# Index projection issued among the last filter sequences of the first stage, two filter layers stacked on 128 partitions, first tokens moved up

## What is computed

```python
# second block: filter network and spectra
hdn = concatenate([t, cos(bands * wpos), -sin(bands * wpos)])      # (1024, 33)
for k, w in enumerate((w_in, w_hid[0], w_hid[1])):                 # 33->64, 64->64, 64->64
    hdn = sin(freq[k] * (hdn @ w + b[k]))
h = (hdn @ w_out).reshape(L, 2, 2, 1024) * exp(-t * deltas)        # two orders, forward and backward
# ... rfft of the two-sided filters: L+1 frequencies, order, channel

# first block: E = 16 meta tokens + 1024 tokens
proj = h @ w_in                       # split into q_a, c_kv, q_idx, k_idx, w_idx, ..., i_h, ...
c = rms_norm(c_kv, kv_norm_g)         # latents (E, 128)
s_h = relu(q_idx @ k_idx.T * 64 ** -0.5)     # 4 index heads
s_idx = sum over heads of s_h * w_idx        # top 256 keys of each query are kept
```

## Time and profile before

| | us |
|---|---|
| median of three executions | 2971.05 (2970.11 to 2971.79) |
| profiled execution, device time | 2972.2 |
| its span in the trace | 2970.2 |
| filter network, until the first filter product on TensorE | 0 to 43.5 |
| sequences 0 to 7 and the stores | 43.5 to 337.5 |
| index projection stage | 337.5 to 386.2 |
| index scores stage | 386.2 to 413.9 |
| TensorE busy, whole span | 2660.5 (90%) |
| VectorE busy, whole span | 1870.5 (63%) |

### The profile page before, as it was taken

How to read it: one execution, slowest core, us unless ns; L and a number is a source line. 1 busy time by engine, 2 the same in 40 slices (tenths; PEclk the granted TensorE clock), 3 DMA queues, 4 the chain that set the end, 5 groups by cost and what they waited for, 6 DMA issues and landing times. The chain is left out here.

```text
span 2970.2 us, 30635 instructions
## 1 busy us (share of the span) xinstructions
PE 2660.5 (90%) x11185; PEld 1832.8 (62%) x11185; DVE 1870.5 (63%) x3013; ACT 927.1 (31%) x1681; POOL 865.8 (29%) x635
## 2 busy tenths in 40 slices
PE   5999789968599979789999999978999997999967
PEld 1444345557356557577787999976788884444456
DVE  6677279997676488657831555544764425887554
ACT  2121131101344333455425656644432220111132
POOL 0000000022121066675632333316532221333235
PEclk9999899989799989899999999998999998999979
DMA  5122301000100054246737231305321123111043
GB/s 165 64 78 85 122 23 36 28 37 1 57 1 1 1 199 135 77 136 219 256 129 232 61 93 48 93 22 169 127 80 43 43 78 152 46 60 60 29 177 106
DMA packets 110703, 265.01 MB, mean 89 GB/s; under 512 B 18387, under 2 KB 37531, under 8 KB 105952
## 3 DMA queue, kind: packets, MB, share of 16 engines
q1 hardware_dynamic: 110560, 263.13, 26.6%
HBM read 202.10 MB, written 60.99 MB: 89 GB/s over the span
## 5 line engine op out<-in xcount | busy, mean ns | idle before, releaser
L313 PE MATMUL psum<-part,part 128*128 128x512 f32 (+1 forms) x1984 | 764.6, 385 | 82.0 <-POOL part L1688 30.1
L314 PE MATMUL psum<-part,part 128*128 128x512 f32 (+1 forms) x1984 | 743.1, 375 | 0.0
L315 PE MATMUL psum<-part,part 128*128 128x512 f32 (+1 forms) x1984 | 741.2, 374 | 0.0
L1688 POOL TENSOR_TENSOR part<-arena,part 128x512 fp32r<-128x512 f32 (+1 forms) x298 | 427.1, 1444 | 631.2 <-ACT part L1682 630.9
L313 PEld LDWEIGHTS psum<-part,part 128*128 128x128 f32 x1984 | 378.4, 191 | 169.4 <-POOL part L1688 71.6
L314 PEld LDWEIGHTS psum<-part,part 128*128 128x128 f32 x1984 | 379.3, 191 | 70.5 <-issue 2.7
L315 PEld LDWEIGHTS psum<-part,part 128*128 128x128 f32 x1984 | 378.0, 191 | 71.7
L1682 ACT ACTIVATE part<-arena 128x512 fp32r<-128x512 f32 (+1 forms) x298 | 181.7, 620 | 364.4 <-PE psum L315 235.1
L221 PE MATMUL psum<-arena 128*128 128x512 f32 (+1 forms) x672 | 231.3, 504 | 17.8 <-DMA arena<-in_w_f 9.9
L1219 POOL TENSOR_TENSOR arena<-arena 128x256 f32<-128x256 f32 x56 | 39.2, 702 | 664.2 <-PE psum L1232 664.2
L2523 DVE TENSOR_REDUCE arena<-psum 128x1 f32<-128x1280 f32 x64 | 95.5, 1492 | 175.9 <-PE psum L2475 175.9
(11 more groups left out here) (326 smaller groups left out, 4112.4 us busy)
## 6 DMA issues: line engine op xcount, KB each, us to landing
arena<-in_ada_w SPq DMA_DIRECT2D x24, 1024.0 KB, 6.2
arena<-in_w_hy SPq DMA_DIRECT2D x40, 512.0 KB, 3.3
scratch_spec<-arena SPq DMA_DIRECT2D x68, 256.0 KB, 2.0
arena<-scratch_spec SPq DMA_DIRECT2D x12, 1024.0 KB, 5.2
arena<-in_w_gate SPq DMA_DIRECT2D x16, 512.0 KB, 4.0
arena<-in_w_out SPq DMA_DIRECT2D x16, 512.0 KB, 3.9
arena<-in_w_mgate SPq DMA_DIRECT2D x16, 512.0 KB, 4.0
arena<-in_w_mout SPq DMA_DIRECT2D x16, 512.0 KB, 3.9
```

Source lines behind the costliest of these rows:

```text
L313: nc.tensor.matmul(acc, a_hi, b_hi, start=start, stop=False)
L314: nc.tensor.matmul(acc, a_hi, b_lo, start=False, stop=False)
L315: return nc.tensor.matmul(acc, a_lo, b_hi, start=False, stop=stop)
L1688: self.K.nc.gpsimd.tensor_tensor(self.lo[s][:, c], self.raw[s][:, c], self.hi[s][:, c].bitcast(F32), ALU.subtract).then_inc(self.split, 1)
```

## The change

Four edits.

1. The stage `stage_index_projection` is gone. Its six products (`index_product(u)`, u = 0..5) are issued in `stage_spectra_tokens`: u = 0 at the start of sequence 6, u = 1 in its middle, u = 2 and u = 3 at the start and in the middle of sequence 7, u = 4 and u = 5 behind it. Each uses bank 6 or 7 and is copied out by ScalarE (`copy_index`). SyncE loads the index weights when the last token product is done, at its place in front of sequence 6. The latents are reloaded in `stage_index_scores`; the index head weights `wi` stay where they are made.
2. The first two layers of the filter network are stacked: both halves of the positions lie on 128 partitions, with block-diagonal weights, so a layer is one product, one reduction of seven instructions and one sine. The last layer stays in two halves. The network is 4 steps instead of 6.
3. Token tile 0 is multiplied in two parts ahead of and between the first filter products, tile 1 right behind them, and the others move up: the tables are now tiles 3, 4, 5, 6, 7 at the start of sequences 1 to 5, and tiles 2 and 8 in the middle of sequences 0 and 5. Sequences 6 and 7 have no token tile; `norm_latents` and its square root move from sequence 7 to sequence 6.
4. The sums and the rest of the second half's output weights move behind `fold_odd(0)` and into sequence 2 on VectorE, their rounding into sequence 1 on ScalarE. The loads are reordered: input and token weights come ahead of the transform's matrices.

```diff
-    AT_START = {0: 0, 1: 2, 2: 4, 3: 5, 4: 6, 5: 7, 6: 8}
-    AT_MIDDLE = {0: 1, 1: 3}
+    AT_START = {1: 3, 2: 4, 3: 5, 4: 6, 5: 7}
+    AT_MIDDLE = {0: 2, 5: 8}
+    INDEX_START, INDEX_MIDDLE, INDEX_END = {6: [0], 7: [2]}, {6: [1], 7: [3]}, [4, 5]
...
+    LAYERS = [(0, 0), (1, 0), (2, 0), (2, 1)]
...
+            def load_index(m):
+                if m == 2:
+                    sp.wait_ge(idx_mm, 2)
+                sp.dma_start(w_idx[m % 2], dram["w_idx"][m, :, :]).then_inc(idx_in[m % 2], 16)
...
+                if k == 6:
+                    sp.wait_ge(i_mm, 9)
+                    load_index(0)
+                    load_index(1)
+                if k == 7:
+                    load_index(2)
...
             rest_of_weights(0)
...
+            take_latent(0)
             for k, (o, h, s) in enumerate(ORDER):
...
-                if k == 0:
-                    sum_weights(1)
+                if k == 2:
                     rest_of_weights(1)
-                if k == 7:
+                if k == 6:
                     norm_latents()
...
+                if k == 0:
+                    take_latent(1)
...
                 fold_odd(K, dve, link, ed, odd, Y, s, y_ready)
+                if k == 0:
+                    sum_weights(1)
...
+            def copy_index(u):
+                act.wait_ge(idx_mm, u + 1)
...
+                for u in INDEX_START.get(k, []):
+                    copy_index(u)
...
-                if k == 7:
+                if k == 6:
                     act.wait_ge(meansq, 1)
                     a(rstd[:, 1:9], rstd[:, 1:9], ACT.Sqrt)
...
-            for q in range(4):
-                hidden_out(0, q)
+            token_products(0, 0)
+            hidden_out(0, 0)
+            hidden_out(0, 1)
+            token_products(0, 1)
+            hidden_out(0, 2)
+            hidden_out(0, 3)
+            token_products(1)
             for k in range(8):
                 if k in AT_START:
                     token_products(AT_START[k])
+                for u in INDEX_START.get(k, []):
+                    index_product(u)
...
+            for u in INDEX_END:
+                index_product(u)
...
-STAGES = [stage_spectra_tokens, stage_index_projection, stage_index_scores, stage_features, stage_hgrn,
+STAGES = [stage_spectra_tokens, stage_index_scores, stage_features, stage_hgrn,
```

More of the change, by code:

```diff
@@ L611, in _ @@
             link(v.memset(K.ones, 1.0))
-            dve.wait_ge(params, 16 * 6)
+            dve.wait_ge(params, 16 * 5)
             def sum_weights(h):
@@ L755, in _ @@
                         copy_values(AT_MIDDLE[k])
+                    for u in INDEX_MIDDLE.get(k, []) if part else []:
+                        copy_index(u)
                     if part and k == 7:
@@ L860 @@
 CT = 15104
+QK = 47312
 FEAT = 16144
@@ L919, in _ @@
         def _(sp):
-            sp.dma_start(causal, K.dram["causal"]).then_inc(loaded, 16)
+            sp.dma_start(causal, dram["causal"]).then_inc(loaded, 16)
+            for dst, src in [(K.cT, dram["cT"]), (K.cN[0:META, 0, :], dram["cN"][0:META, 0, :]),
+                             (K.cN[:, 1:9, :], dram["cN"][:, 1:9, :]), (K.vN[0:META, 0, :], dram["vN"][0:META, 0, :]),
+                             (K.vN[:, 1:9, :], dram["vN"][:, 1:9, :])]:
+                sp.dma_start(dst, src).then_inc(back, 16)
+            sp.wait_ge(back, 16 * 5)
         @block.tensor
```

185 lines of the change are left out of this document (103 added, 82 removed).

## The result

| | before | after |
|---|---|---|
| median | 2971.7 us (5 runs, 2970.1 to 2976.8) | 2958.0 us (5 runs, 2952.8 to 2960.5) |
| ratio | | 0.9945 [0.9927, 0.9962] |
| span of the profiled execution | 2970.2 us | 2957.6 us |
| start of the score products | 386.3 | 370.75 (forecast 365.9) |
| start of the selection behind them | 414.0 | 400.3 |

The kernel is faster by 13.7 us by the medians (0.46%) and by 0.55% [0.38, 0.73] by the ratio, which is 16 us; 20 were forecast. The time lies inside the range of 2941 to 2965 and 7 us above the predicted 2951. In the trace 15.5 us are gained at the start of the scores, 13.7 at the start of the selection, 12.6 at the end.

The account below looks back on a forecast made before the run. TensorE, busy 90% of the span, was taken as the bound, with the time to gain at the stage's two ends. 9.7 us up to O and 10.7 behind it gave 20.4 us off, 2951 us, range 2941 to 2965.

Parts of the forecast that it names:

- the clock stays down: Rival: short products at the start do not raise TensorE's clock; about +9 us there, +4 at the end, 2964 us; chance 0.25.
- O: End of the odd part of sequence 5, forecast at 262.4 us against 272.1 before, 9.7 us earlier.
- The filter network: Start of the stage: stacking saves two reductions, so the first filter product can start at 36.6 us, 6.9 us earlier.
- The first tokens: Sequence 0: half of tile 0 hidden under the network's wait; 5.1 us idle remain, odd part ends at 99.6 against 109.3.
- The end: From O to the index scores: 103.5 us against 114.2, with new idle times of 5.1, 9.2 and about 4 us.
- The scores: Index scores stage: reload of latents and values, 3.1 MB, costed at nothing beside the score products; 8 us without that cover.
- The later stages: Behind the index scores: untouched, so the same 20 us were taken off the median.
- the clock stays up: Rival: the clock stays up behind the short idle times, so 5.1, 1.3 and 2.5 us fall away; 2942 us; chance 0.15.
- The holes are not filled: Rival: index product 0's weights land 13 us after O, delaying sequence 6's folds; 13 us lost, 2964 us; chance 0.06.
- Slower: Rival: the later stages, started 20 us earlier, lose 1% of clock and the gain is gone; 2975 us; chance 0.04.

Follow-up runs that it names:

- fill_idles: Changed kernel with unread products filling two TensorE idle stretches, ahead of the first filter product and of sequence 1's third filter pair; 2951.4 us, ratio 0.9924.
- index_own_stage: Changed kernel with the index projection put back in a stage of its own, the roots staying in sequence 6; 2961.7 us, ratio 0.9969.
- load_first: Changed kernel with SyncE's index weight loads issued ahead of the stores of the odd part of sequence 5; 2951.1 us, ratio 0.9923.
- causal_alone: Changed kernel with SyncE issuing the five reloads of the scores stage only once the causal mask has landed; 2957.3 us, ratio 0.9951.
- roots_first: Changed kernel with ScalarE's square roots ahead of its copies of the odd part of sequence 5; 2936.3 us, ratio 0.9893.
- mask_early: Changed kernel with the causal mask loaded in the stage before the scores, at the start of sequence 7; 2953.3 us, ratio 0.9944.
- tile0_whole: Changed kernel with all of token tile 0 ahead of the first filter product; 2952.2 us, ratio 0.9934.
- stack_only: Kernel before with only the changed kernel's stacked filter network; 2964.6 us, ratio 0.9981.

## Why the prediction was right, and where its steps were off

The sign, the places and the mechanisms came as told; the amount was two thirds of the forecast by the medians (13.7 of 20). The time by itself does not choose between the forecast and its strongest rival: 2958.0 lies 7 us from 2951 and 6 from the 2964 of *the clock stays down*. The trace does. Step by step, with O at 265.6:

- **The filter network**: first filter product 36.05, forecast 36.6. Right.
- **The first tokens**: the wait for latent 0 was sized at 2.0 us and measured 1.21. But the step took the upper clock for the whole start and added the lower one only behind its last wait (until 75.6 in the forecast, 79.41 in the trace). The clock fell in the 5.14 us ahead of the filter products and again at 52.4, and 12.8 us of the 30.5 ran at 1.2 GHz: the first transform started at 66.55 and not at 61.7, 4.85 late. The step had the wait in it but no price beside it, though it charged exactly that price (5.1) to the next wait. At 79.41 the idle time was 4.01 and not 5.1, and the odd part ended at 103.05 against 99.6. So O came 3.2 us late, at 265.6 and not 262.4; fill_idles, with both holes filled, reached it at 259.8.
- **The end**: the weights' wait 4.99 (5.1; the terms named for it, 0.2, 0.6 and 3.9, give 4.7, and the trace has another 0.4 between the end of the last copy and the issue of the load), index product 0 ended at O + 13.9 (13.5), VectorE resumed at O + 16.2 (15.7), the even part of 6 at O + 26.6 (26.1) with 9.50 idle (9.2), the filter pair at O + 40.5 (39.9), but with 2.01 idle ahead of it and not 4: the even part had taken until then at the lower clock. Index product 1 behind it ran at that clock once more. Scores at O + 105.2 against 103.5: 1.6 too few for the clock. The list that the forecast gives of what its 10.7 us are made of adds up to 13.0 at least; the time was not taken from it. The table load took 1.28 us and the first root began 0.02 us behind its end, so the drain that the Trainium skill gives (page "ScalarE: Activation LUTs", section "What ACT_TABLE_LOAD costs") was not paid here.
- **The scores**: the stage was taken as unchanged, with the reload costed at nothing. The reload cost nothing that the runs show: from the start of the score products to the selection it is 27.6 us in fill_idles, with the reload beside them, and 27.6 in index_own_stage, without. The mask came 1.8 us later, in the company of a packet of instructions, which fill_idles was spared. This term was missing.
- **The later stages** were taken as equal; in the profiled execution they took 1.1 us more.

3.2 + 1.6 + 1.8 + 1.1 = 7.7, which is the 20.4 forecast less the 12.6 of the span, but for rounding.

The rivals: the clock neither stayed up nor down. It fell in or right behind each of the four waits of 4 us or more (5.14, 4.01, 4.99, 9.50), and some 2 us behind the one of 2.01, and rose again within 12 us of work. The forecast had it for all of these but the first. The 9 us that *the clock stays down* put on the start were 3.2. In *the clock stays up* the forecast takes back 1.3 us for index product 0, for which its sum has 1.5; it changes nothing that was concluded. *The holes are not filled* did not come; load_first shows that its concern, the queue behind the stores, was the 5 us of the forecast and no more. *Slower* through the later stages falls: started up to 45 us earlier, they took 2548 to 2557 us in thirteen executions, with no trend. The executions of one kernel differed by 8 us all the same, those of causal_alone by 14, more than the spread of three runs of before had led me to think.

## What to carry over

An idle time of TensorE can cost more than its length: in the changed kernel the holes of 5.14, 4.01, 4.99, 9.50 and 2.01 us were followed by 4.8, 4.6, 1.8, 3.0 and 3.3 us that TensorE lost to the lower clock. So removing a wait can give back more than its length (roots_first, 17 us for 11.5 us of waits), and harmless work in it can pay. A step that others wait for is to stand where its input is ready, not where its stage's order puts it: the square root and the weight loads were ready a whole odd part earlier than they were issued. Where a trace's gain at one point is not there at a later one, look at the granted clock between the two before looking for a new wait.

## What the runs showed that I had not expected

- The granted clock falls amid full work too. In the sequences behind the first, with no wait over 1.1 us, the profiled executions of the changed kernel and of causal_alone spent nothing at 1.2 GHz, that of before 3.4 us, of mask_early 9.8, of tile0_whole 10.1, of stack_only 16.8, at places that differ from kernel to kernel, and what stood behind moved by half of it. What decides the place no run here shows.
- With one packet of the instruction queue, 0.02 MB, under way, VectorE started on a mask of 64 KB 0.5 to 2.0 us later than without. In causal_alone the last sixteenth of it (nine of 144 packets) moved 0.3 us or more behind the rest. One DMA engine shared by both would explain it; that was not shown.
